# The second block's router beside the output tiles, and a layer norm applied per token on turned rows

## What is computed

```python
# second_block, after the hybrid mixer m
x = layer_norm_2(ALPHA * x + m, ln1_g, ln1_b)          # mean, variance over 1024 channels, eps 1e-5
f = hierarchical_moe(x, w_rg, b_rg, w_re, b_re, w_up, w_down)
x = layer_norm_2(ALPHA * x + f, ln2_g, ln2_b)

def hierarchical_moe(x, ...):
    group_p = softmax(xf @ w_rg + b_rg)                 # 4 groups, the best one is taken
    exp_logits = xf @ w_re + b_re                       # 16 experts, the best two of the group
    ...                                                 # gates, SwiGLU experts of width 256
```

## Time and profile before

| | |
|---|---|
| median of three executions | 2556.64 us |
| profiled execution | 2553.45 us |
| its span, first to last instruction | 2551.7 us |
| TensorE matmuls busy | 2355.5 us (92%) |
| VectorE busy | 1127.1 us (44%) |
| ScalarE busy | 912.1 us (36%) |
| GpSimd busy | 268.4 us (11%) |
| mean granted clock of TensorE | 0.979 |

### The profile page before, as it was taken

One profiled execution on the slowest core, in us unless ns is written; L12 is line 12 of the kernel. 1 busy time (PEld: TensorE's weight loads), 2 busy tenths in 40 slices (PEclk: granted clock), 3 DMA queues, 4 the chain that ended last, 5 costly groups with the idle time before them and its releaser, 6 DMA issues. The chain is left out here.

```text
span 2551.7 us, 31078 instructions
## 1 busy us (share of the span) xinstructions
PE 2355.5 (92%) x12693; PEld 1491.1 (58%) x12693; DVE 1127.1 (44%) x1688; ACT 912.1 (36%) x1222; POOL 268.4 (11%) x245
## 2 busy tenths in 40 slices
PE   6989799999988989799999989999999999989997
PEld 5744544333336735544334338887888777767776
DVE  5985312222215974422222225656611012459997
ACT  4246211111114256211111126666622234247775
POOL 0000100000000000100000005000355433300100
PEclk8999899999999999899999999999999999989999
DMA  9701589999999503399999994523223421159995
GB/s 360 278 1 53 211 332 428 429 428 429 429 427 371 213 1 128 158 399 428 428 429 428 429 411 133 165 83 99 70 84 91 136 78 54 50 188 382 372 370 213
DMA packets 196716, 650.40 MB, mean 255 GB/s; under 512 B 12144, under 2 KB 110718, under 8 KB 169726
## 3 DMA queue, kind: packets, MB, share of 16 engines
q1 hardware_dynamic: 192884, 637.98, 63.9%
q0 software_dynamic: 2592, 7.87, 0.8%
q10 hardware_dynamic: 1130, 2.99, 0.3%
HBM read 641.99 MB, written 8.39 MB: 255 GB/s over the span
## 5 line engine op out<-in xcount | busy, mean ns | idle before, releaser
L878 PE MATMUL ps<-ring,hy 128*64 128x512 f32 x992 | 225.1, 596 | 37.7 <-DMA ring<-in_w_up 26.1
L1389 DVE TENSOR_TENSOR scr<-scr,ps 128x512 f32<-128x512 f32 x32 | 22.0, 688 | 500.4 <-PE ps L878 500.4
L878 PE MATMUL ps<-ring,scr 128*64 128x512 f32 x992 | 224.5, 595 | 15.8 <-DMA ring<-in_w_up 14.7
L1656 POOL TENSOR_TENSOR raw_r<-raw,w_high 128x512 fp32r<-128x512 f32 (+1 forms) x160 | 189.4, 1218 | 433.7 <-ACT w_high L1924 433.7
L908 PE MATMUL ps<-ring,scr 128*64 128x512 f32 x1024 | 227.0, 596 | 2.9 <-ACT scr L1100 2.7
L1679 PE MATMUL ps<-x_high,w_high 128*128 128x512 f32 x464 | 186.6, 402 | 3.5 <-DVE y L2320 3.5
L1681 PE MATMUL ps<-x_high,raw_r 128*128 128x512 f32 x464 | 184.3, 397 | 0.0
L1680 PE MATMUL ps<-xT_r,w_high 128*128 128x512 f32 x464 | 183.4, 395 | 0.0
L2745 DVE TENSOR_TENSOR ring_r<-ring,ring_high 128x2048 fp32r<-128x2048 f32 x77 | 172.9, 2287 | 18.3 <-ACT ring_high L2668 18.2
L878 PEld LDWEIGHTS ps<-ring,hy 128*64 128x64 f32 x992 | 68.2, 137 | 188.7 <-issue 122.2
L1177 DVE SCALAR_TENSOR_TENSOR one_hot_T<-h_tok,convw,one_hot_T 128x512 f32<-128x512 f32 x240 | 166.4, 748 | 1.8
(11 more groups left out here) (597 smaller groups left out, 4530.8 us busy)
## 6 DMA issues: line engine op xcount, KB each, us to landing
ring<-in_w_up SPq DMA_DIRECT2D x64, 2048.0 KB, 25.6
ring<-in_w_down SPq DMA_DIRECT2D x64, 2048.0 KB, 20.4
ring<-in_w_gate SPq DMA_DIRECT2D x60, 2048.0 KB, 23.0
ring<-in_w_up SPq DMA_DIRECT2D x56, 1024.0 KB, 6.8
ring<-in_w_ada SPq DMA_DIRECT2D x22, 2048.0 KB, 14.3
ring<-in_w_down SPq DMA_DIRECT2D x28, 1024.0 KB, 6.7
raw<-in_w_in SPq DMA_DIRECT2D x24, 1024.0 KB, 5.1
raw<-in_w_in SPq DMA_DIRECT2D x20, 512.0 KB, 5.2
```

What stands on the lines that cost most here:

```text
L878: mm = pe.matmul(ps[CAP * half:CAP * (half + 1), 1 + j // 2, :], x_e[j % 2][:, at_x:at_x + CAP], weights[:, k, half * HALF:(half + 1) * HA ...
L1656: part = pool.tensor_tensor(dst[:, a:a + 2], src[:, a:a + 2], high[:, a:a + 2].bitcast(F32), ALU.subtract)
```

## The change

In `second`:

- The channel sums are taken over four tiles only (`SHIFT_KT = 4`), each one tile behind instead of two. VectorE subtracts this shift from all eight tiles of `xT` after output tile 4; the last three output tiles are added to it afterwards.
- The router's weights are loaded here (SP, ahead of the first `w_o` chunk). VectorE multiplies them by the layer norm's gain and bias and sums them up, between the rebuilding of `xT` and the first addition.
- TensorE multiplies the shifted, unnormalised tokens by the weighted router and adds a column of ones (the sum of the channels) and the squares, which ScalarE makes: tiles 0 to 4 before output tile 7, the rest behind it. ScalarE loads the table of the root at the end.

In `sparse`:

- The whole layer norm ahead of the router is gone. Mean, variance and logits of each token are worked out by ten small VectorE instructions on the turned logits.
- `keep_rows` applies scale and shift per token. GpSimd multiplies the rows by the gain and adds the bias (eight instructions of 128x1024), and sends them to memory on its own queue. Gain and bias of the first 128 tokens are applied behind the one-hot gather by ScalarE (eight instructions and two copies).
- The slot lists stand behind unit 0; the splits of the first weights are placed later in ScalarE's and VectorE's orders; a third turned tile comes before the group sums on TensorE, in other banks.
- The first seven weight chunks are loaded without a wait, and the last layer norm's rows are loaded before chunk 10, once GpSimd has made the rows.

```diff
@@ second, SP
+                if i == CH_O:
+                    sp.wait_ge(m_y, 2 * KT)
+                    sp.dma_start(w_g[:, :, 0:4], A["w_rg_2"][0].rearrange("(k p) n -> p k n", p=P)).then_inc(wg_in, 16)
+                    sp.dma_start(w_g[:, :, 4:20], A["w_re_2"][0].rearrange("(k p) n -> p k n", p=P)).then_inc(wg_in, 16)
...
@@ second, TensorE
+            def logits(kt):
+                if kt <= SHIFT_KT:
+                    pe.wait_ge(x_shifted, kt + 1)
+                else:
+                    pe.wait_ge(wo_used, kt + 1)
+                for g in range(TT):
+                    pe.matmul(ps[GROUP * g:GROUP * (g + 1), 7, 0:P], w_gained[:, kt, :], xT[:, kt, g * P:(g + 1) * P], start=(kt == 0), stop=False)
+                pe.wait_ge(o_sq, kt + 1)
+                for g in range(TT):
+                    mm = pe.matmul(ps[GROUP * g:GROUP * (g + 1), 7, 0:P], sq_column, o_sq_buf[:, kt % 4, g * P:(g + 1) * P], start=False, stop=(kt == KT - 1))
+                mm.then_inc(o_used, 1)
...
-            for dt in range(KT + 2):
-                if dt < KT:
-                    if dt >= 4:
-                        pe.wait_ge(wo_used, dt - 3)
-                    feature_tile(2 + dt % 4, CH_O + dt // 2, dt % 2, tiles(y_high), tiles(y_low), (y_low_ready, 0) if dt == 0 else None).then_inc(wo_mm, 1)
-                if dt >= 2:
-                    pe.wait_ge(wo_used, dt - 1)
-                    mm = norm_sum(xT, dt - 2)
-            mm.then_inc(l_sum, 1)
+            for dt in range(KT):
+                if dt >= 4:
+                    pe.wait_ge(wo_used, dt - 3)
+                feature_tile(2 + dt % 4, CH_O + dt // 2, dt % 2, tiles(y_high), tiles(y_low), (y_low_ready, 0) if dt == 0 else None).then_inc(wo_mm, 1)
+                if 1 <= dt <= SHIFT_KT:
+                    pe.wait_ge(wo_used, dt)
+                    mm = norm_sum(xT, dt - 1)
+                if dt == SHIFT_KT:
+                    mm.then_inc(l_sum, 1)
+                    pe.wait_ge(w_sum_ready, 1)
+                    pe.matmul(ps[:, 6, 0:2 * N_LOGITS], ones[:], w_sums, start=True, stop=True)
+                if dt == KT - 2:
+                    for kt in range(SHIFT_KT + 1):
+                        logits(kt)
+            for kt in range(SHIFT_KT + 1, KT):
+                logits(kt)
@@ second, ScalarE
+            for kt in range(KT):
...
+                act.activation(o_sq_buf[:, kt % 4, :], xT[:, kt, :], ACT.Square).then_inc(o_sq, 1)
+            act.activation(small[:, 99:100], eps, ACT.Sqrt)
@@ second, VectorE, behind the rebuilding of xT
-            for dt in range(KT):
-                dve.wait_ge(ax_ready, dt + 1)
+            dve.wait_ge(wg_in, 64)
...
+            step(dve.tensor_tensor(w_gained[:, :, 0:N_LOGITS], w_g, gain, ALU.mult))
+            step(dve.tensor_tensor(w_biased, w_g, bias, ALU.mult))
+            step.settle()
+            step(dve.reduce_sum(w_sums[:, 0:N_LOGITS], w_gained[:, :, 0:N_LOGITS].rearrange("p k n -> p n k"), AX_X))
+            step(dve.reduce_sum(w_sums[:, N_LOGITS:2 * N_LOGITS], w_biased.rearrange("p k n -> p n k"), AX_X))
...
+            for dt in range(SHIFT_KT + 1):
+                dve.wait_ge(ax_ready, dt + 1)
+                add_output(dt)
+            dve.wait_ge(l_sum, 1)
+            dve.wait_ge(ax_ready, KT)
+            dve.wait_ge(wo_used, SHIFT_KT + 1)
+            for kt in range(KT):
+                dve.scalar_tensor_tensor(xT[:, kt, :], ps[:, 0, :], -1.0 / (SHIFT_KT * P), xT[:, kt, :], ALU.mult, ALU.add).then_inc(x_shifted, 1)
+            for dt in range(SHIFT_KT + 1, KT):
+                dve.wait_ge(x_shifted, dt + 1)
+                add_output(dt)
@@ sparse, SP
+            sp.dma_start(gain_row, A["ln1_g_2"].to_broadcast([P, D])).then_inc(first_rows_in, 16)
+            sp.dma_start(bias_row, A["ln1_b_2"].to_broadcast([P, D])).then_inc(first_rows_in, 16)
...
+                if q == RING + 3:
+                    sp.wait_ge(rows_made, TT)
+                    sp.dma_start(gain_row, A["ln2_g_2"].to_broadcast([P, D])).then_inc(g_rows, 16)
@@ sparse, GpSimd
+            pool.wait_ge(first_rows_in, 32)
+            step = Steps(pool, p3_step)
+            for t in range(TT):
+                pool.wait_ge(row_kept, 2 * (t + 1))
+                step(pool.tensor_tensor(row_out[t], xtok[:, t, :], gain_row, ALU.mult))
+                step.settle()
+                pool.tensor_tensor(row_out[t], row_out[t], bias_row, ALU.add).then_inc(rows_made, 1)
+                pool.wait_ge(rows_made, t + 1)
+                pool.dma_start(rows[t], row_out[t]).then_inc(rows_out, 16)
@@ sparse, ScalarE
+                    act.activation(xtok[:, t, half * HALF:(half + 1) * HALF], ps[:, ROW_BANKS[2 * t + half], :], ACT.Identity,
+                                   bias=shift[:, t:t + 1], scale=rstd[:, t:t + 1]).then_inc(row_kept, 1)
...
+            def keep_first_tokens():
+                for half in range(2):
+                    act.wait_ge(xt_mm, half + 1)
+                    for b in range(4):
+                        kt = 4 * half + b
+                        step(act.activation(first_x[:, kt, :], ps[:, 6 + half, b * P:(b + 1) * P], ACT.Identity, bias=col(C_L1B + kt), scale=col(C_L1G + kt)))
+                    step.settle()
+                    act.activation(xh[0][:, 4 * half:4 * half + 4, :], first_x[:, 4 * half:4 * half + 4, :], ACT.Copy).then_inc(xh_ready, 1)
@@ sparse, VectorE
+            op(dve.tensor_scalar(mean, turned[:, :, N_LOGITS], 1.0 / D, None, ALU.mult))
...
+            split_rest("up0", 0)
...
+            token_half(0, 0)
+            split_rest("up1", 0)
+            token_half(0, 1)
...
-            tokens_rest(0)
+            split_rest("up0", 1)
             dve.wait_ge(disp_mm, 1)
```

More of the change, by code:

```diff
@@ L1699, in norm_sum @@
             def norm_sum(x, kt):
-                return pe.matmul(ps[:, 0, :], ones[:], x[:, kt, :], start=(kt == 0), stop=(kt == KT - 1))
+                return pe.matmul(ps[:, 0, :], ones[:], x[:, kt, :], start=(kt == 0), stop=(kt == SHIFT_KT - 1))
+            def logits(kt):
[9 more added lines that the diff above has]
+                mm.then_inc(o_used, 1)
             def kv_tile(i):
@@ L2439, in sparse @@
     stored = [sem(f"stored{i}") for i in range(2)]
+    mean, square, rstd, shift = (V["moments"][:, TT * i:TT * (i + 1)] for i in range(4))
+    first_x = xT[:, :, 0:P]
     d3_step = sem("d3_step")
@@ L2560, in _ @@
             groups = V["group"]
-            pe.matmul(ps[:, 3, 0:16], V["upper"], groups, start=True, stop=False)
+            pe.matmul(ps[:, 6, 64:80], V["upper"], groups, start=True, stop=False)
             for t in range(1, TT):
-                mm = pe.matmul(ps[:, 3, 0:16], ones[:], V["gpad"][:, 12 - 4 * t:28 - 4 * t], start=False, stop=(t == TT - 1))
+                mm = pe.matmul(ps[:, 6, 64:80], ones[:], V["gpad"][:, 12 - 4 * t:28 - 4 * t], start=False, stop=(t == TT - 1))
             mm.then_inc(rank_mm, 1)
@@ L2567, in _ @@
             mm.then_inc(count_mm, 1)
-            for t in range(2, TT):
-                pe.wait_ge(row_kept, 2 * (t - 1))
-                turn_rows(t)
+            turn_rows(3)
             pe.wait_ge(row_kept, 2 * TT)
@@ L2578, in _, with slot_lists @@
                 mm.then_inc(xt_mm, 1)
-            pe.wait_ge(disp_ready, 1)
-            for t in range(TT):
-                mm = pe.matmul(ps[:, 2, 0:6 * TILES], hot[:, t, :], V["mov"][:, t * 6 * TILES:(t + 1) * 6 * TILES], start=(t == 0), stop=(t == TT - 1))
-            mm.then_inc(disp_mm, 1)
+            def slot_lists():
+                pe.wait_ge(disp_ready, 1)
+                for t in range(TT):
+                    mm = pe.matmul(ps[:, 2, 0:6 * TILES], hot[:, t, :], V["mov"][:, t * 6 * TILES:(t + 1) * 6 * TILES], start=(t == 0), stop=(t == TT - 1))
+                mm.then_inc(disp_mm, 1)
             def turn_tokens(i):
@@ L2668, in split @@
                 act.activation(high[q], raw[q], ACT.Copy).then_inc(w_split, 1)
-            split("up0", 0)
-            split("up1", 0)
-            for kt in range(KT):
-                act.wait_ge(l_norm, kt + 1)
-                act.activation(xT[:, kt, :], xT[:, kt, :], ACT.Identity, bias=col(C_L1B + kt), scale=col(C_L1G + kt)).then_inc(l_ready, 1)
             def keep_rows(t):
@@ L2678, in keep_rows @@
                     act.wait_ge(row_mm, 2 * t + half + 1)
[L2679 to L2682 removed]
+                    act.activation(xtok[:, t, half * HALF:(half + 1) * HALF], ps[:, ROW_BANKS[2 * t + half], :], ACT.Identity,
+                                   bias=shift[:, t:t + 1], scale=rstd[:, t:t + 1]).then_inc(row_kept, 1)
+            act.wait_ge(l_inv, 1)
             keep_rows(0)
+            keep_rows(1)
             act.wait_ge(g_sub, 1)
             act.activation(ex, ex, ACT.Exp).then_inc(g_exp, 1)
[L2686 removed]
+            keep_rows(2)
             act.wait_ge(e_sub, 1)
             act.activation(inner, inner, ACT.Exp).then_inc(e_exp, 1)
[L2689 to L2693 removed]
+            keep_rows(3)
```

(20 more changed lines are left out.)

124 lines of the change are left out of this document (60 added, 64 removed).

## The result

| | before | after |
|---|---|---|
| median (six executions each) | 2553.89 us | 2574.49 us |
| profiled execution, span | 2553.45, 2551.7 us | 2570.17, 2568.4 us |
| mean granted clock of TensorE | 0.979 | 0.974 |

The ratio is 1.0071, with a 95% interval from 1.0058 to 1.0085: the change costs 18 us (15 to 22). One of the six executions of the changed kernel took 8303 us; nothing here explains it. It stays out of the ratio, but the median in the table counts it; without it the median is 2573.26 us.

A forecast was written before the change was run, and what follows sets the result against it. TensorE, with work in 92% of the span, was taken as the bound, so its waits count: +10.3 up to the last block, +0.1 to unit 1, +2.0 clock, sum +12.4 on the median 2556.64, so 2569.0 us; range 2558 to 2575.

The forecast's parts named there:

- The stall, 6.6: Output tiles: TensorE waits behind tile 1 for VectorE's first addition; 6.6 us, bounds 5.9 to 7.3.
- The clock behind it, 2.5: Output tiles, after TensorE's wait behind tile 1: half clock for a while, a loss of 2.5 us (1.7 to 3.4).
- The work ahead of the last tile's end, +1.6: Output tiles: one norm sum less, but router sums, square sums and a weight sum added on TensorE; +1.6 us.
- The last tile to S, -0.4: From the last output tile's end to the start of the last block: 3.3 us instead of 3.7, so -0.4.
- Unit 1 at S+41.8: Last block: unit 1 of the experts starts 41.8 us after the block begins, against 41.65 before; +0.1 us.
- S+26: Last block: with all engines free, unit 1 would start 26 us after the block begins, 15.4 us earlier than before.
- The clock in unit 1, +2.0: Last block: TensorE idles ahead of unit 1 and starts it at half clock; +2.0 us (1.7 to 3.4).
- "Just covered": the gathers: Last block: second gather lands 56 us after the block begins, TensorE needs it at 58; no term in the sum.
- Rival 3: Last block: row writes on GpSimd's queue land late (12.6 to 14.7 us), TensorE waits; +17, 2574 us; chance 0.12.
- Rival 1: Last block: the lock between GpSimd and VectorE is milder, the gathers decide; +5, 2561.5 us; chance 0.17.
- Rival 4: Output tiles: VectorE adds tile 0 before tile 1 ends, so no stall; +3.3, 2560 us; chance 0.07.
- Rival 2: Last block: VectorE free and gathers early, the whole 15.4 us counts; -5 to -9, 2549 to 2552 us; chance 0.07.

The follow-up runs named there:

- e1: Changed kernel with the early norm sums moved behind later output tiles and the router's constants behind VectorE's second addition; 1.0027 times the kernel before.
- e5: e1 with ScalarE's dummy square root, which loads its table, moved ahead of the square of the last tile but one; 1.0022 times the kernel before.
- e2: Changed kernel without GpSimd's eight row steps (gain and bias left out of the rows for tiles 1 to 6); 1.0001 times the kernel before.
- e4: Changed kernel with each of GpSimd's eight row steps cut into four of 256 columns; 1.0100 times the kernel before.
- e10: e5 with row work on VectorE, its gain and bias loaded before the first weight chunks, the last norm's before the tenth; 0.9992 times the kernel before.
- e11: e10 with the last two of the five row steps behind the first tokens moved behind the slot lists; 1.0007 times the kernel before.
- e3: Changed kernel with GpSimd's row work made to wait until VectorE has made the slot lists; 1.0116 times the kernel before.
- e9: Changed kernel with the last norm's gain and bias loaded ahead of the tenth weight chunk instead of the eleventh; 1.0058 times the kernel before.
- e7: e5 with the rows' gain and bias loaded ahead of the first two weight chunks instead of behind them; 1.0008 times the kernel before.

## Why the prediction was right, and where it was short

The forecast, slower, with its mechanism, held; the size was short. It forecast +12.4 us, and the ratio says 18 (15 to 22). The forecast of 2569.0 us looks closer to the 2574.5 measured than that, since the three executions it started from have a median 2.75 us above that of all six. By its own steps:

- **The stall, 6.6.** Measured 6.63. The constants took 2.5 (2.3 taken).
- **The clock behind it, 2.5.** Tile 2 and its sum take 8.35 us instead of 6.43, so 1.9. Together with the stall 8.5; e1 gave 8.7 back.
- **The work ahead of the last tile's end, +1.6.** What is left of the 10.6 us by which that end moved is 2.1.
- **The last tile to S, -0.4.** Measured +0.4, and this step failed in its choice: I knew both ends (the last router sums, or the table load) and took a value near the first. ScalarE's timeline after the change:

```profile
2260.64 1.28 ACT L2159 ACT_TABLE_LOAD   x1
2261.94 0.20 ACT L2159 ACTIVATE small<-const 128x1 f32<-128x1 f32 x1
```

The load starts right behind the last square, the root ends at 2262.14, and the last block begins 1.0 us behind it. e5 shows that it was the load: moved, it gives 1.0 us back. The Trainium skill (ScalarE: Activation LUTs, What ACT_TABLE_LOAD costs) adds a drain of 1.38 us; this trace shows none, the load is followed by the root 0.02 us after its end. (With such a drain my upper end would have been +1.7, not the +1.0 that I gave.)

- **Unit 1 at S+41.8.** Measured 41.3. GpSimd began at S+11.1 (10.7) and ended at S+37.6 (37), the lists were ready at S+39.0 (39.5). The end of GpSimd's work was right by luck in part: the pushes from VectorE's big steps took 3.8 us, not 6.0, and the DMA issues and waits between the steps 3.9, not 1.5. The reason was the right one: without the row work unit 1 starts at S+28.5 (e2), 2.5 later than my S+26. The exclusive way to SBUF of the Trainium skill (SBUF — State Buffer, Terms) fits the held steps of 2.0 to 2.8 us; e4 adds that the loser may miss the gap between two instructions (3.25 us for a product of 0.17).
- **The clock in unit 1, +2.0.** Unit 1 takes 8.37 us instead of 5.57: 2.8.
- **"Just covered": the gathers.** True for the second gather, which I had worked out, and wrong as a sum. TensorE waited 1.6 us for tile 2's tokens and 0.9 for tile 6's, 2.3 more than before. Every variant has such waits, from 1.0 us in all (e10) up to 8.5 (e11) and 27.7 (e3), so the term belongs in the sum. Tile 2's gather takes 7.8 us from issue to landing, as before; it is issued later, 3.2 us after TensorE begins to turn the hidden values of unit 4 instead of 2.0. Timelines of ScalarE, VectorE and GpSimd after the change, then of GpSimd before it:

```profile
2345.09 1.92 ACT L2727 ACTIVATE ring_high<-ring 128x2048 fp32r<-128x2048 f32 x1 [2.87 <-DMA ring<-in_w_up]
2347.04 2.29 DVE L2802 TENSOR_TENSOR ring_r<-ring,ring_high 128x2048 fp32r<-128x2048 f32 x1 [2.50 <-ACT ring_high L2727]
2349.25 1.28 DVE L2915 SCALAR_TENSOR_TENSOR yt<-xg,ps 128x512 f32<-128x512 f32 x2
2351.28 0.94 POOL L2575 DMA_INDIRECT xg<-token_rows,route_i  x1 [40.47 <-DVE yt L2915]
```

```profile
2335.73 0.94 POOL L2507 DMA_INDIRECT xg<-token_rows,route_i  x1 [41.14 <-DVE yt L2845]
```

The issue waits for `yt` on VectorE, `yt` stands behind a weight split, and the split waits for ScalarE, which waits 2.9 us for a weight chunk (1.5 before). So this wait for a gather begins with a late weight chunk. Why the chunk is late isn't settled: in e9, with the last norm's rows earlier, ScalarE waits 1.9 us for it, the issue comes 2.3 us after that turn begins and tile 2's wait is 0.9, but tile 4's gather takes 8.4 us to land and TensorE waits 1.2 us there.

Rival 3 fell with its premise: GpSimd's row writes landed in 2.9 to 6.5 us (median 3.9), not 12.6 to 14.7. In e2, where they are issued earlier, they took 7.2 to 11.5. Rival 1's chain is real but needs an early unit 1; e3 and e11 are that case. Rival 4 is e1, which had to be built. Rival 2 needed what e2 shows, no row work, and even that is level with the kernel before (1.0001). Two sums there were slightly off: -9 us is 2548, not 2549, and the chances given add up to slower 0.81, same 0.12.

Left open: the ratio puts the change at 18 us (15 to 22), the traces at 15.9 behind T0 and 0.8 ahead of it. Their sum lies within the interval, so nothing is needed to explain the rest.

## What to carry to other kernels

Work that is moved to an idle engine isn't free if its instructions hold up those of the engine on the path: look in the trace for steps that run longer beside it, price the work by the wait per instruction, and compare with doing it on the other engine (here eight steps of 1.2 us on VectorE beat eight of 2.4 on GpSimd by 8 us). A reduction that is pulled one step forward waits for everything its producer still has queued; look at that queue first. When one wait is removed, the next is often just behind it (lists, then gathers), so work out all chains to the same point and give what is "just covered" a term in the sum (here, e3, e4 and e11 aside, TensorE waited 1.0 to 3.4 us in all for gathers).

## What I had not expected of the hardware

- The hold between VectorE and GpSimd reaches steps that seem to have one wide input only: four one-hot columns of 128x128 took 4.96 us instead of 0.88 (e7). Two of the four cases in the earlier trace rows were such steps already, scalings, though my text spoke of two SBUF inputs. The router's reductions, and its steps that read PSUM, stayed under 0.3 us throughout.
- It doesn't share evenly: with four GpSimd instructions of 256 columns back to back a VectorE product of 0.17 us takes 0.39 to 0.66 us, held for one of them, or 3.25, held for all four (and a step of 2.29 takes 5.30).
- Behind the wait for the lists unit 1 runs at 1.2 GHz at first (0.63 us a pass, granted clock 0.50 from 2304 to 2310), which costs 2.8 us in the changed kernel. In e7 the long wait and the slow passes fall into unit 0, and unit 1, with no wait ahead of it, takes 6.3 us instead of 8.1. That is one pair of traces (e5 and e7), and not a rule.
